# Head sums and their spread in 16 partitions with full-width products, instead of 128 partitions in four 32-wide groups

## The reference

```
kk = (kf * k_k).reshape(B, L, H, N)
kk = kk * rsqrt(maximum(sum(kk * kk, axis=-1, keepdims=True), 1e-24))
...
mean = mean(y, axis=-1, keepdims=True)
var = mean(square(y - mean), axis=-1, keepdims=True)
y = (y - mean) * rsqrt(var + LNX_EPS) * lnx_w + lnx_b
```

## Time and profile before

| | us |
|---|---|
| median of 3 runs | 1219.25 |
| lowest and highest | 1216.72, 1220.33 |
| time of the profiled execution | 1220.33 |
| its span in the trace | 1218.5 |
| PE busy, of the span | 91% |
| DVE, ACT, POOL busy | 68%, 52%, 20% |

### The profile page before, as it was taken

One profiled execution on the slowest core, in us unless ns is written; L12 is line 12 of the kernel. 1 busy time (PEld: TensorE's weight loads), 2 busy tenths in 40 slices (PEclk: granted clock), 3 DMA queues, 4 the chain that ended last, 5 costly groups with the idle time before them and its releaser, 6 DMA issues.

```text
span 1218.5 us, 23564 instructions
## 1 busy us (share of the span) xinstructions
PE 1113.4 (91%) x9448; PEld 1001.9 (82%) x9448; DVE 828.9 (68%) x1087; ACT 638.1 (52%) x925; POOL 240.8 (20%) x192
## 2 busy tenths in 40 slices
PE   5889899999979997999689999979999799999986
PEld 5787788998759866998579889859998799998765
DVE  5687466687866659565756867775757777775774
ACT  4675355655625466333346556543444566764552
POOL 1000023453620005914113435520000100000000
PEclk9998999999979998999799999988999899999998
DMA  7522367778654510000357787753565365566200
GB/s 276 168 70 70 118 201 251 256 243 272 199 171 139 173 57 2 4 4 3 121 177 246 246 268 251 252 163 121 174 193 187 104 205 178 169 205 190 88 1 35
DMA packets 81850, 190.47 MB, mean 156 GB/s; under 512 B 5808, under 2 KB 6080, under 8 KB 81648
## 3 DMA queue, kind: packets, MB, share of 16 engines
q1 hardware_dynamic: 72896, 157.31, 39.0%
q0 software_dynamic: 7584, 27.53, 7.5%
q10 hardware_dynamic: 1296, 4.58, 1.0%
HBM read 188.34 MB, written 1.05 MB: 155 GB/s over the span
## 4 chain that ended last, share of the span: by engine, by line
PE 79%; DVE 11%; ACT 3%; issue 3%; POOL 2%; DMA 2%; ACTq 0%; POOLq 0%; DVEq 0%; SPq 0%
PE bank L1790 13%; PE bank L1792 13%; PE bank L1791 13%; PE bank L1773 4%; PE bank L1775 4%; PE bank L1774 4%; PE bank L1975 4%; PE bank L1976 4%; PE bank L1977 4%; PE bank L2118 3%; POOL mod_all L498 1%; PE bank L2016 1%; PE bank L1814 1%; DVE w_lo L1128 1%; PE bank L2236 1%
## 5 line engine op out<-in xcount | busy, mean ns | idle before, releaser
L1128 DVE TENSOR_TENSOR w_lo<-raw,w_hi 128x1024 fp32r<-128x1024 f32 x296 | 391.9, 1340 | 247.7 <-ACT w_hi L642 247.4
L642 ACT ACTIVATE w_hi<-raw 128x1024 fp32r<-128x1024 f32 x296 | 312.0, 1058 | 351.0 <-PE bank L1792 179.7
L1790 PE MATMUL bank<-act_hi,w_hi 128*128 128x256 f32 x1392 | 394.1, 283 | 13.4 <-DMA bk<-in_rwkv_a_dram 7.6
L1792 PE MATMUL bank<-act_hi,w_lo 128*128 128x256 f32 x1392 | 392.9, 282 | 0.0
L1791 PE MATMUL bank<-act_lo,w_hi 128*128 128x256 f32 x1392 | 392.9, 282 | 0.0
L1790 PEld LDWEIGHTS bank<-act_hi,w_hi 128*128 128x128 f32 x1392 | 264.3, 190 | 15.7 <-DMA bk<-in_rwkv_a_dram 7.9
L1791 PEld LDWEIGHTS bank<-act_lo,w_hi 128*128 128x128 f32 x1392 | 264.4, 190 | 0.8 <-issue 0.2
L1792 PEld LDWEIGHTS bank<-act_hi,w_lo 128*128 128x128 f32 x1392 | 264.3, 190 | 0.0
L498 POOL TENSOR_TENSOR mod_all<-mod_all,mod_w 128x1024 f32<-128x1024 f32 x42 | 109.8, 2613 | 144.3 <-ACT mod_w L811 143.4
L474 POOL TENSOR_SCALAR stat<-stat 128x1 f32<-128x1 f32 x16 | 9.0, 563 | 608.9 <-ACT xn L660 608.4
L1975 PE MATMUL bank<-w_hi,ff_hi 128*128 128x512 f32 x256 | 102.6, 401 | 5.7 <-DVE ff_lo L1326 5.7
(11 more groups left out here) (302 smaller groups left out, 1489.2 us busy)
## 6 DMA issues: line engine op xcount, KB each, us to landing
raw<-in_mlp_w_up_dram SPq DMA_DIRECT2D x64, 512.0 KB, 4.8
raw<-in_mlp_w_down_dram SPq DMA_DIRECT2D x64, 512.0 KB, 4.4
raw<-in_dil_w_in_dram SPq DMA_DIRECT2D x64, 512.0 KB, 4.2
mod_w<-in_w_mod_dram POOLq DMA_DIRECT2D x48, 512.0 KB, 4.2
raw<-in_conv_w_in_dram SPq DMA_DIRECT2D x32, 512.0 KB, 3.7
raw<-in_rwkv_w_rkv_dram SPq DMA_DIRECT2D x24, 512.0 KB, 4.4
raw<-in_dsa_w_in_dram SPq DMA_DIRECT2D x16, 512.0 KB, 5.0
raw<-in_dsa_w_o_dram SPq DMA_DIRECT2D x8, 512.0 KB, 3.7
```

Source lines behind the costliest of these rows:

```text
L642: act.activation(w_hi[:, slot, :], raw[:, slot, :], ACT.Copy).then_inc(hi_ready, 1)
L1128: dve.tensor_tensor(w_lo[:, slot, :], raw[:, slot, :], w_hi[:, slot, :].bitcast(F32), ALU.subtract).then_inc(lo_ready, 1)
L1790: pe.matmul(dst, w_hi[:, slot, at], hi[:, kt, :], start=begin, stop=False, skip_group_check=True)
L1792: mm = pe.matmul(dst, w_lo[:, slot, at], hi[:, kt, :], start=False, stop=end, skip_group_check=True)
```

## The change

The sums of all 16 heads go into 16 PSUM rows: for each pair a product with a stationary matrix of 16 columns (`head_of` becomes [128, 8, 16]), and the eight products accumulate in one place. `per_head` and a new `root_head` have 16 partitions. The spread is one product for each pair with 16 rows of `rows_of` [16, 8, 128], written bank by bank, with a semaphore increment for each bank, and in `rwkv_mid` the first two banks wait only for two pairs of sigmoids. `rows_of` leaves `const` (which loses 256 columns there and gains 64 for `head_of`) and becomes an input of its own, 16 rows of 1024 fp32. It is loaded as a sixth LoRA load by POOL, into the first 16 partitions of `scale_row`, and PE waits for six loads. The load of the final norm's gain moves from the start to the beginning of the second MLP on ACT.

```
-    head_of = np.zeros((P, 2, 32), np.float32)
-    rows_of = np.zeros((P, 2, P), np.float32)
+    head_of = np.zeros((P, PAIRS, HEADS), np.float32)
+    for pair in range(PAIRS):
+            head_of[h * RN:(h + 1) * RN, pair, 2 * pair + h] = 1.0
+    rows_of[:HEADS] = head_of.transpose(2, 1, 0)
...
-        per_head = sb("per_head", [P, SEQ])
+        per_head = sb("per_head", [HEADS, SEQ])
+        root_head = sb("root_head", [HEADS, SEQ])
...
+        rows_of = scale_row[0:HEADS, :].rearrange("h (a p) -> h a p", p=P)
...
+                pool.dma_start(rows_of, A["rows_of"].rearrange("h (a p) -> h a p", p=P)).then_inc(lora_loaded, 16)
...
-                act.dma_start(scale_row[:, :], A["final_norm"].partition_broadcast(P)).then_inc(scale_loaded, 16)
...
+                if l:
+                    act.wait_ge(spread_full, 4)
+                    act.dma_start(scale_row[:, :], A["final_norm"].partition_broadcast(P)).then_inc(scale_loaded, 16)
...
-                act.activation(per_head[:, :], per_head[:, :], ACT.Sqrt).then_inc(rw_root, 1)
+                act.activation(root_head[:, :], per_head[:, :], ACT.Sqrt).then_inc(rw_root, 1)
...
-                dve.reciprocal(per_head[:, :], per_head[:, :]).then_inc(rw_inverse, 1)
+                dve.reciprocal(root_head[:, :], root_head[:, :]).then_inc(rw_inverse, 1)
...
-                dve.tensor_scalar(per_head[:, :], bank[7][:, 0:SEQ], 1e-24, None, ALU.max).then_inc(sums_ready, 1)
+                dve.tensor_scalar(per_head[:, :], bank[7][0:HEADS, 0:SEQ], 1e-24, None, ALU.max).then_inc(sums_ready, 1)
...
-                    dve.wait_ge(kk_spread, 1)
+                    dve.wait_ge(kk_spread, b + 1)
...
-                    dve.wait_ge(spread_full, 1)
+                    dve.wait_ge(spread_full, b + 1)
...
-                pe.wait_ge(lora_loaded, 16 * 5)
+                pe.wait_ge(lora_loaded, 16 * 6)
...
-            def head_sums(b, values, at=slice(0, SEQ)):
-                for par in range(2):
-                    for g in range(4):
-                        mm = pe.matmul(bank[b][32 * g:32 * g + 32, at], head_of[:, par, :], values[:, 2 * g + par, at], start=par == 0, stop=par == 1)
+            def spread(b, pairs):
+                for j, pair in enumerate(pairs):
+                    mm = pe.matmul(bank[b][:, j * SEQ:(j + 1) * SEQ], rows_of[:, pair, :], root_head[:, :], start=True, stop=True)
+                return mm
...
-                head_sums(7, R["pinv"]).then_inc(kk_sums, 1)
+                for pair in range(PAIRS):
+                    mm = pe.matmul(bank[7][0:HEADS, 0:SEQ], head_of[:, pair, :], R["pinv"][:, pair, :], start=pair == 0, stop=pair == PAIRS - 1)
+                mm.then_inc(kk_sums, 1)
...
-                pe.wait_ge(lora2_ready, 4)
-                spread(0).then_inc(kk_spread, 1)
+                for b in range(4):
+                    pe.wait_ge(lora2_ready, 2 + 2 * (b // 2))
+                    spread(b, (2 * b, 2 * b + 1)).then_inc(kk_spread, 1)
...
-                    head_sums(4, R["sg"], slice(half * P, (half + 1) * P)).then_inc(var_full, 1)
+                    at = slice(half * P, (half + 1) * P)
+                    for pair in range(PAIRS):
+                        mm = pe.matmul(bank[4][0:HEADS, at], head_of[:, pair, :], R["sg"][:, pair, at], start=pair == 0, stop=pair == PAIRS - 1)
+                    mm.then_inc(var_full, 1)
...
-                spread(4).then_inc(spread_full, 1)
+                for b in range(4):
+                    spread(4 + b, (2 * b, 2 * b + 1)).then_inc(spread_full, 1)
```

More of the change, by code:

```diff
@@ L98, in shape_constants @@
     head_ones = np.kron(np.eye(2), np.ones((RN, RN)))
-    in_group = np.arange(P) % 32
-    head_of = np.zeros((P, 2, 32), np.float32)
-    rows_of = np.zeros((P, 2, P), np.float32)
-    for par in range(2):
+    head_of = np.zeros((P, PAIRS, HEADS), np.float32)
+    for pair in range(PAIRS):
         for h in range(2):
-            head_of[h * RN:(h + 1) * RN, par, 2 * par + h] = 1.0
-            rows_of[:, par, h * RN:(h + 1) * RN] = (in_group == 2 * par + h)[:, None]
+            head_of[h * RN:(h + 1) * RN, pair, 2 * pair + h] = 1.0
+    rows_of = np.zeros((P, PAIRS, P), np.float32)
+    rows_of[:HEADS] = head_of.transpose(2, 1, 0)
     parts = {
@@ L118, in shape_constants @@
         "head_of": head_of,
-        "rows_of": rows_of,
         "ones": np.ones((P, P), np.float32),
@@ L129, in shape_constants @@
     parts_bf = {"ident_bf": ident, "causal": causal, "dil_mask": dil}
-    return parts, parts_bf
+    return parts, rows_of, parts_bf
 def program(nc, A, out):
-    parts, parts_bf = shape_constants()
+    parts, _, parts_bf = shape_constants()
     with ExitStack() as keep:
@@ L196, in program @@
         before_mask = view["before_mask"].rearrange("p (m t) -> p m t", m=2)
-        head_of = view["head_of"].rearrange("p (a h) -> p a h", a=2)
-        rows_of = view["rows_of"].rearrange("p (a m) -> p a m", a=2)
+        head_of = view["head_of"].rearrange("p (a h) -> p a h", a=PAIRS)
         def xn_plan(t):
@@ L1597, in rwkv_out @@
                 dve.wait_ge(var_full, 2)
-                dve.tensor_scalar(per_head[:, :], bank[4][:, 0:SEQ], 1.0 / RN, LNX_EPS, ALU.mult, ALU.add).then_inc(sums_ready, 1)
+                dve.tensor_scalar(per_head[:, :], bank[4][0:HEADS, 0:SEQ], 1.0 / RN, LNX_EPS, ALU.mult, ALU.add).then_inc(sums_ready, 1)
                 dve.wait_ge(offset_ready, 4)
@@ L2391, in laid_out @@
 def laid_out(inputs):
-    parts, parts_bf = shape_constants()
+    parts, rows_of, parts_bf = shape_constants()
     arrays = {name: np.asarray(value) for name, value in inputs.items() if np.size(value)}
@@ L2400, in laid_out @@
     arrays["const_bf"] = np.concatenate([v.reshape(P, -1) for v in parts_bf.values()], 1)
+    arrays["rows_of"] = rows_of[:HEADS].reshape(HEADS, -1)
     return arrays
```

## The result

The changed kernel took 1226.17 us (median of 5 executions, 1222.83 to 1228.92), the kernel before 1219.68 in the same comparison (1216.72 to 1221.93): a ratio of 1.0054, 95% interval 1.0035 to 1.0073. The change makes the kernel slower by half a per cent. Over all 146 later executions of the kernel before its median is 1221.0. One of them was at 1428.94; all others lie between 1216.55 and 1228.43.

A forecast was written before the change was run, and what follows sets the result against it. The prediction took the tensor engine (PE), busy 91% of 1218.5 us, as the bound. Terms +0.4 + 2.1 + 0 + 0 - 2.1 + 0 made +0.4 us; it said 1219.9 us, range 1216.3 to 1223.8.

The forecast's parts named there:

- the second spread: Spread at 587.65 us, behind the scan: PE's unbroken work raises the clock before the output projection; -2.1 us.
- The start: Kernel start: one 512 KB load and 96 KB of const less, landing under PE work; 0 us, also in the second MLP.
- The sixth LoRA load: Before the r, k, v projections: PE waits for a sixth load's landing; +0.4 us, between 0 and 2.25.
- rival 2: Before the projections: the sixth load costs a full step of 2.25 us instead of 0.4; time 1221.5; chance 12%.
- The head sums: At 448 us: sums run one after another, 3.57 us instead of 1.07, delaying the root; +2.1 us.
- The spread at 455 us: Ahead of the scan: 3.57 us instead of 1.15, hidden by DVE's scans; price 0.
- rival 4: Sums and spreads: weight loads do not overlap in one set of rows; sum +4.2 us, 1223.5; chance 5%.
- The variance sums: At 580 us: two halves of 1.78 us instead of 0.64, hidden behind DVE's splits; price 0.
- rival 1: Second spread: small spreads do not raise the clock, projection 1.2 us late at half clock; +3.7 us, 1223.0; chance 12%.
- Rival 3: Before the second spread: clock does not fall; -3.3 us there instead of -2.1, sum -0.8, 1218.4; chance 13%.
- Rival 5: Head sums: new sums run side by side after all, first place costs nothing; sum -1.7 us, 1217.6; chance 3%.

The follow-up runs named there:

- e1: Changed kernel with the 16 rows of rows_of loaded at the start on ACT's queue, PE waiting for five LoRA loads; 1225.77 us against 1221.22, ratio 1.0040.
- e13: Changed kernel plus an unused tile of 64 bytes a partition behind the constants; 1223.48 us, ratio 1.0023 to the kernel before.
- e14: Kernel before plus an unused tile of 64 bytes a partition behind the constants; 1215.92 us, ratio 0.9961.
- e17: Changed kernel plus the unused 64 bytes and the LoRA wait moved to the first LoRA product; 1214.22 us against 1219.74, ratio 0.9948.
- e18: Repeat of e16: kernel before plus 64 unused bytes and the late LoRA wait; 1210.43 us against 1219.74, ratio 0.9928.
- e3: Kernel before with only the change's DMAs: sixth LoRA load waited for, final-norm load moved to the second MLP; 1220.98 us, ratio 1.0011.
- e11: Kernel before with only the LoRA wait moved from ahead of all projections to the first LoRA product; 1217.69 us against 1221.21, ratio 0.9965.
- e16: Kernel before plus 64 unused bytes and the LoRA wait moved to the first LoRA product; 1209.51 us against 1221.2, ratio 0.9924.
- e4: As e1, but new sums and spread only ahead of the scan, four-group form behind it; 1222.76 us against 1221.22, ratio 1.0011.
- e8: As e1, but new sums and spread only behind the scan, four-group form ahead of it; 1222.29 us against 1220.54, ratio 1.0014.
- e2: As e1, but sums with 128 output columns (112 zero) and spreads reading 128 rows; 1217.00 us against 1221.22, ratio 0.9970.
- e12: e2 with the LoRA wait moved to the first LoRA product; 1217.14 us, ratio 0.9955 to the kernel before.
- e6: As e1, but spreads read 128 rows, those beyond 16 set to ones by GpSimd; sums keep 16 columns; 1238.09 us, ratio 1.0131.
- e9: e6 with the ones set by DVE just ahead of per_head and no wait for GpSimd; 1227.68 us against 1221.21, ratio 1.0052.
- e5: As e1, but sums write 128 output columns while spreads read 16 rows; 1217.95 us against 1220.54, ratio 0.9984.
- e15: Kernel before plus an unused tile of 32 bytes a partition behind the constants; 1219.89 us, ratio 0.9999.
- e10: As e2, but sums of 32 output columns and spreads reading 32 rows; 1224.72 us against 1221.21, ratio 1.0022.
- e7: As e2, but sums of 64 output columns and spreads reading 64 rows; 1217.51 us against 1220.54, ratio 0.9982.

## Why the prediction was wrong

It gave 1219.9 and a range to 1223.8. **The step that failed is the second spread, the term of -2.1 us:** PE's unbroken work there was to bring the clock up before the output projection, and did not. In its place the runs show +0.8 us or more. Between new and old form the runs give 6.5 us in the first comparison, 4.6 in e1, 7.6 between e13 and e14, and 3.8 between e17 and e18. The forecast had +0.4.

The traces give the change's cost stage by stage. "First sum" is the start of the first product of the head sums ahead of the scan, "root" and "second root" are ACT's two square roots, and "48th" is the start of the 48th product of the output projection. In us:

| traces | first sum to root | root to L2161's products | first sum to second root | second root to projection | second root to 48th | first sum to 48th |
|---|---|---|---|---|---|---|
| before | 2.01 | 35.8 | 136.8 | 8.5 | 21.4 | 158.2 |
| old form: e3, e11, e14, e16, e18 | 2.01 | 34.3 | 135.7 | 8.5 | 21.5 to 21.6 | 157.2 to 157.3 |
| new form: after, e1, e17 | 4.11 | 35.0, 35.0, 35.7 | 138.1, 138.5, 138.7 | 9.7, 9.4, 9.1 | 22.4 | 160.5, 160.9, 161.1 |
| new form: e13 | 4.11 | 36.7 | 139.7 | 9.2 | 22.4 | 162.0 |
| new ahead of the scan only: e4 | 4.11 | 35.0 | 138.1 | 8.5 | 21.9 | 160.0 |
| new behind it only: e8 | 2.01 | 34.3 | 135.7 | 9.9 | 23.7 | 159.4 |
| 128 columns and rows: e2, e12 | 4.11 | 35.8 | 138.9 | 7.9 | 19.0 | 157.9 |

Point by point:

- **The start, the final norm's load.** Priced at 0. e3 has both: 1.0011, no cost seen. Right.
- **The sixth LoRA load, +0.4.** PE starts at 362.71 against 362.94, and e1, without the load there, is no faster beyond the noise. Right within 0.4, and rival 2 is out.
- **The head sums, +2.1.** 3.63 us instead of the forecast 3.57. The root comes 2.01 us after the first sum in every trace with the old form, and 4.10 to 4.16 in every one with the new, save e6 and e9 with their added wait: +2.1. Right. At the second root the shift against the old form's usual 135.7 us has grown to 2.4 to 3.9, since the old form gets 1.0 us back on the way at half clock (next point) and the new one less. So this place costs 0.3 to 1.8 us more than forecast. The single trace of before, with 136.8, hides that.
- **The spread at 455 us, price 0.** 3.69 us, as worked out by the row, with 16 weight loads of 3.31 us beside the products. The Trainium skill's rule of rival 4 (TensorE: Matmul & The Clock Gate, "Part 3: Packing small matmuls", "The mechanism"), that a load overlaps only where the row group differs, would have made it 6.9; the trace disagrees with that sentence, though the same section also names loads into a background weight buffer as ones that go ahead of running products. The text let L2083 keep its 7.15 us. That assumption failed: 13.77 us. The price of 0 held within 1 us all the same, save in e5 and e13. From the root to the scan's L2161 products the kernel before, at full clock, takes 35.8 us (450.09 to 485.93), and e3, e8, e11, e14, e16 and e18, the old form at half clock, 34.3 (e15 35.8). The new form at half clock takes 35.0 in after, e1, e4 and e10, and at full clock, with wider spreads, 35.8 in e2, e7 and e12. Where the clock fell already within the spread, it takes 36.7 (e5, e13); there the half clock does cost. Timelines of DVE and POOL show how the old form gains at half clock, before and then e3:

```profile
472.25 4.54 POOL L536 TENSOR_TENSOR uv<-uv,v_mean 64x1024 f32<-64x1024 f32 x2
472.64 2.39 DVE L1490 TENSOR_TENSOR rr<-rr,cum 128x512 f32<-128x512 f32 x1
474.95 2.38 DVE L1486 TENSOR_TENSOR bk<-a,pinv 64x512 f32<-64x512 f32 x1
475.08 1.97 PE L2118 MATMUL bank<-kk,bk 64*64 64x64 f32 x32 [7.61 <-DVE rr L1490]
```

```profile
472.83 0.68 DVE L1496 TENSOR_TENSOR rr<-rr,cum 128x512 f32<-128x512 f32 x1
473.43 0.67 DVE L1492 TENSOR_TENSOR bk<-a,pinv 64x512 f32<-64x512 f32 x1
...
476.09 4.70 POOL L539 TENSOR_TENSOR uv<-uv,v_mean 64x1024 f32<-64x1024 f32 x2 [3.73 <-PE bank L2098]
```

With vT late, GpSimd's uv operation comes later and no longer runs beside DVE's rr and bk, which take 0.68 us instead of 2.4. The scan starts 1.4 us later after the root (26.4 against 25.0), and by L2161 it is 1.5 us ahead.
- **The variance sums, price 0.** 3.67 us for both halves, hidden behind DVE's splits; per_head at 584.31 against 584.38. Right.
- **The second spread, -2.1.** This is the step that failed: "PE stays busy" was to bring the clock up before the projection. It did not. The spread took 6.94 us at half clock and the projection's first 3.6 us ran at half clock, 4.2 before. From the second root to the projection are 9.1 to 9.9 us with the narrow new form, against 8.5 in every trace of the old one; to the 48th product, where part of this is made up, it is +0.8 (e8: +2.1). That is rival 1 in kind, PE late and the clock not back in time, and e1 and e6, which there differ in the rows of the spread, show it: with 16 rows the clock came back 10.8 us after the spread's start, with 128 rows after 4.1, before the projection. With 128 rows the stage is 2.6 us shorter than with the old form (e2, e12), so a gain of the forecast's size was there to be had, but with spreads of 128 rows. Rival 1 had 12%. One size was low in both forecast and rival: 16 instructions at half clock were put at 6.9 us, while twice the row's 0.223 gives 7.1, and e8 took 7.19.

Of the two theories, B had the sizes about right (sums +2, second spread +1, the clock of L2079 mostly hidden), and A the reason for the second spread. By the stages the change costs 3.2 to 3.9 us in after, e1 and e17, and 4.8 in e13, each against the old form at the same place of the tiles; measured 6.5, 4.6, 3.8 and 7.6. For e4 the stages give 2.7 and for e8 2.1; measured 1.5 and 1.75. A ratio's interval is about 2 us either way here, so most of the cost is found; what is left over in the first comparison and in e13, about 3 us, is in no stage that these traces name, and stays open. Rival 3 was half right without help: the clock was indeed still full at 587, but then fell under the spread. Rival 5 is out.

That the time landed 6.3 us over the forecast has three parts: 2.9 us of the second spread (-2.1 forecast, +0.8 found), 0.3 to 1.8 us of the first place, and the rest that stays open. My base was also low, since the three times shown were fortunate ones (median 1219.25 against 1221.0 over 146).

Why e6 (1238.1) and e9 (1227.7) differ by 10 us at the same place of the tiles stays open as well; against e1 their place should cost 4176 x 1.7 + 1440 x 0.9 = 8.4 us and the added wait 2.7, and the second spread gives back 3.7, which makes 1233.

## What to carry to other kernels

Count on a clock that rises only if a row shows it rising behind the same kind of work; a forecast gain that needs it deserves a coin's chance, not the main case. When a variant changes the size of a tile, first compare the distance of unrelated instructions in both traces: here a table 56 bytes longer gave about half of e2's gain or more, and the first reading put all of it on the width of the products. A wait that is added to make a variant correct can cost by itself: e6's and e9's kept a table load from its cover. And one trace is one draw: take the stage's length from several before calling a long instruction a cost, or the only trace at hand the usual one.

## What was not expected of the hardware

- The granted clock fell to half while PE was busy without a gap. Ahead of L2079 (or its like) it was half in all five traces with sums and spreads of 16 (after, e1, e4, e13, e17), in e5 (spread of 16) and e10 (32), in seven of eight with the packed form, and full in all five with spreads of 64 or 128 rows (e2, e6, e7, e9, e12). The stage up to L2161 did not get longer by it, save in e5 and e13.
- Behind the scan the granted clock was full before the projection's first product in all four traces with spreads of 128 rows, and half in all eight with new spreads of 16 to 64.
- The clock also differs from trace to trace elsewhere: in the first projection (26 to 34 us) it was 1.00 in the traces of before, after and e2, and 0.57 in e9's:

```profile
26.00:34.00 8.00, 8.00 (x44) 8.00 (x44) 3.29 (x7) 1.25 (x2) 0.00 (x0) 0.57 0.75 259
```

- Over 145 executions of the kernel before, the mean granted clock lay between 0.949 and 0.965, and the time went down by 0.76 us for each 0.001 more (correlation -0.72).
- The distance of fp32 products changed with the place in SBUF at which the tiles behind the constants begin: 118.3, 116.7 to 117.4, 120.0 and 120.0 ns for 256 columns at `act_hi` = 96, 160, 128 and 224 modulo 256 bytes; 233.3, 233.3, 227.3 and 234.2 for 512; at 32 (e10) 117.6 for 256 columns. No rule was found.
- DVE's 64x512 and 128x512 operations took 0.68 us alone and 2.4 beside a GpSimd operation of 64x1024.
